# A three-block model on one core: first vectors by quarters of columns, expert weights in pieces of 16 KB, and the last scatter moved into the next stage

## The reference

```
def first_block(x, c, ctx, c_ctx, mod_w, mod_b, norm1_g, norm2_g, ...):
    for i in range(2):
        mod = silu(c) @ mod_w[i] + mod_b[i]          # 1024 -> 6 * 1024
        sh1, sc1, g1, sh2, sc2, g2 = split(mod, 6)
        mod_c = silu(c_ctx) @ mod_w[i] + mod_b[i]    # the same for the context
        h = rmsnorm(x, norm1_g[i]) * (1 + sc1) + sh1     # hc likewise
        y, yc = mixer_i(h, hc, w_qkv, w_o, ...)
        x = x + g1 * y                               # xc likewise, in layer 0
        h2 = rmsnorm(x, norm2_g[i]) * (1 + sc2) + sh2
        x = x + g2 * hier_moe(h2, ...)
    return rmsnorm(x, final_g)

def hier_moe(t, ...):     # group by argmax, 2 of the group's 8 experts by top-2
    # 32 experts, each: hidden = silu(x @ w_gate[e]) * (x @ w_up[e]); hidden @ w_down[e]
    # w_gate, w_up: 1024 x 512, w_down: 512 x 1024, each 2 MiB
```

## Time and profile before

| | us |
|---|---|
| median of 3 runs | 2894.34 (2894.28 to 2894.62) |
| profiled execution, its own time | 2893.44 |
| span of the profiled execution | 2891.6 |
| TensorE busy | 2449.8 (85%) |
| VectorE / ScalarE / GpSimd busy | 982.0 (34%) / 550.9 (19%) / 165.6 (6%) |
| DMA moved | 599.06 MB, mean 207 GB/s |

### The profile page before, as it was taken

The page is one execution under the profiler, slowest core; times in us unless marked ns, Lnnn a source line. Parts: engine busy times, 40 slices in busy tenths (PEclk is TensorE's granted clock), DMA queues, the critical chain, the costliest instruction groups (busy, mean ns, idle before and its releaser), DMA issues. The chain is left out here.

```text
span 2891.6 us, 30373 instructions
## 1 busy us (share of the span) xinstructions
PE 2449.8 (85%) x12101; PEld 1302.0 (45%) x12101; DVE 982.0 (34%) x2138; ACT 550.9 (19%) x1222; POOL 165.6 (6%) x270
## 2 busy tenths in 40 slices
PE   6999888795987777697986987777796787999999
PEld 2444356453644334344744644343343653444444
DVE  3221177654322222475734222222365342000000
ACT  3000077311100000115711100000122541000000
POOL 0000000001211111000001111111000000000000
PEclk9999999996999999898997999999898888999999
DMA  8454310507999999611057999999600123222110
GB/s 312 163 193 172 132 46 1 207 29 316 419 419 420 419 419 417 250 44 34 1 199 321 417 418 419 419 418 408 220 15 4 48 73 116 69 76 87 58 58 29
DMA packets 128449, 599.06 MB, mean 207 GB/s; under 512 B 21508, under 2 KB 23820, under 8 KB 73008
## 3 DMA queue, kind: packets, MB, share of 16 engines
q1 hardware_dynamic: 117744, 576.05, 50.3%
q0 software_dynamic: 10560, 21.01, 1.9%
HBM read 580.12 MB, written 30.51 MB: 211 GB/s over the span
## 5 line engine op out<-in xcount | busy, mean ns | idle before, releaser
L1706 PE MATMUL moe_down<-moe_wd,moe_hid_t 128*64 128x512 f32 x1024 | 238.8, 609 | 57.0 <-DMA moe_wd<-in_moe_w_down 43.9
L1661 PE MATMUL moe_gate<-moe_wg,moe_xg_t 128*64 128x256 f32 x1984 | 232.9, 388 | 55.2 <-DMA moe_wg<-in_moe_w_gate 53.7
L1661 PE MATMUL moe_up<-moe_wu,moe_xg_t 128*64 128x256 f32 x1984 | 228.9, 383 | 59.2 <-DMA moe_wu<-in_moe_w_up 59.2
L398 PE MATMUL qkv_acc<-qkv_w,a_buffer 128*128 128x512 f32 x576 | 256.2, 598 | 1.4 <-DVE a_buffer L473 1.2
L2890 PE MATMUL mlp_acc<-m_h,mlp_w 128*128 128x512 f32 x512 | 224.4, 599 | 11.4 <-DMA mlp_w<-in_w_up 9.4
L2905 PE MATMUL mlp_acc<-mlp_w,mlp_u_t 128*128 128x512 f32 x512 | 220.0, 592 | 1.4 <-DVE mlp_u_t L2925 1.4
L1661 PEld LDWEIGHTS moe_gate<-moe_wg,moe_xg_t 128*64 128x64 f32 x1984 | 148.6, 139 | 158.6 <-DMA moe_wg<-in_moe_w_gate 90.0
L1661 PEld LDWEIGHTS moe_up<-moe_wu,moe_xg_t 128*64 128x64 f32 x1984 | 147.0, 138 | 137.2 <-DMA moe_wu<-in_moe_w_up 78.3
L398 PEld LDWEIGHTS qkv_acc<-qkv_w,a_buffer 128*128 128x128 f32 x576 | 107.4, 191 | 132.7 <-issue 123.9
L2890 PEld LDWEIGHTS mlp_acc<-m_h,mlp_w 128*128 128x128 f32 x512 | 97.7, 192 | 137.7 <-issue 127.9
L1706 PEld LDWEIGHTS moe_down<-moe_wd,moe_hid_t 128*64 128x64 f32 x1024 | 73.7, 139 | 178.0 <-issue 126.1
(11 more groups left out here) (406 smaller groups left out, 2958.0 us busy)
## 6 DMA issues: line engine op xcount, KB each, us to landing
moe_wg<-in_moe_w_gate SPq DMA_DIRECT2D x64, 2048.0 KB, 34.6
moe_wu<-in_moe_w_up SPq DMA_DIRECT2D x64, 2048.0 KB, 34.5
moe_wd<-in_moe_w_down SPq DMA_DIRECT2D x64, 2048.0 KB, 34.7
qkv_mod_w<-in_mod_w SPq DMA_DIRECT2D x48, 1024.0 KB, 4.9
mlp_w<-in_w_up SPq DMA_DIRECT2D x8, 2048.0 KB, 9.1
mlp_w<-in_w_down SPq DMA_DIRECT2D x8, 2048.0 KB, 7.9
qkv_w<-in_a_w_qkv SPq DMA_DIRECT2D x12, 1024.0 KB, 9.2
moe_results<-dif_zeros SPq DMA_DIRECT2D x12, 512.0 KB, 5.2
```

What stands on the lines that cost most here:

```text
L398: mm = nc.tensor.matmul(acc[i % 4][:], h_t[:, k, t * P:(t + 1) * P], w[:, c % w_ring, k, :], start=(k == 0), stop=(k == KD - 1))
L1661: mm = nc.tensor.matmul(acc[b][halves[f], 0:HF], x_t[:, k, c, :], w[:, c, k, f * HF:(f + 1) * HF], start=(c, k) == (0, 0), stop=(c, k) == ...
L1706: mm = nc.tensor.matmul(down[b][halves[c], :], hid_t[:, k, h, :], wd[z][:, 2 * h + k, c * NCHUNK:(c + 1) * NCHUNK], start=(k, h) == (0, 0) ...
```

## The change

**A. Entry of layer 0.** Group 0's vectors are computed by quarters of 256 shift and 256 scale columns: slice z holds all 8 eighths of the contraction for 256 columns (1 MiB in 1 KB pieces), slices 0 to 5 land in the still unused buffers of q and k, and 6 and 7 in the ring. SyncE's order of loads is new; rows are loaded in pairs of tiles. The norm's sums run for tiles 0 to 3 and then 4 and 5. TensorE weaves quarters, turns of the quarters' rows, hats and the products of the first four items together. `store_rows(0)` goes. The other 40 slices are spread over items 4 to 35.

```
-    due = [later * (i + 1) // len(items) for i in range(len(items))]
+    due = [max(0, later * (i - 3) // (len(items) - 4)) for i in range(len(items))]
+    ahead = 4
+    stats = [slice(0, 4), slice(4, NT)]
...
+                if g == 0:
+                    u, side = k // 2, k % 2
+                    n0 = side * D + u * 2 * P
+                    sp.dma_start(part_slice(z), src[:, :, n0:n0 + 2 * P]).then_inc(
+                        mod_in[z % ring] if z >= 6 else early_in[z], 16)
+                    return
...
+            load_rows(0)
+            sp.dma_start(e["ident"][:], e["c_ident"]).then_inc(s["g_in"], 16)
+            load_rows(1)
...
+            load_slice(0)
+            load_slice(1)
             sp.wait_ge(s["bias_clear"], 1)
             load_bias(0)
-            load_bias(1)
-            for z in range(KD):
-                load_slice(z)
-            load_chunk(0)
+            load_half(0, 0)
+            load_slice(2)
+            load_slice(3)
+            load_rows(2)
+            load_slice(4)
+            load_slice(5)
+            load_half(0, 1)
+            load_slice(6)
+            load_slice(7)
...
+            def use_quarter(u):
+                if u >= 2:
+                    pe.wait_ge(s["mod_read"], u - 1)
+                for z in (2 * u, 2 * u + 1):
+                    pe.wait_ge(mod_in[z % ring] if z >= 6 else early_in[z], 16)
+                for k in range(KD):
+                    for j in range(4):
+                        mm = nc.tensor.matmul(mod_acc[u % 2][32 * j:32 * j + 32, 0:P], act_v[:, k, :],
+                                              part_slice(2 * u + j // 2)[:, k, quarter(j % 2)],
+                                              start=(k == 0), stop=(k == KD - 1))
...
+            def first_products(u, some):    # matmuls k = 2u, 2u+1 of the items `some`
+                for i in some:
+                    c, t = items[i]
+                    for k in (2 * u, 2 * u + 1):
...
+                        mm = nc.tensor.matmul(acc[i][:], h_t[:, k, t * P:(t + 1) * P], w[:, 0, k, :],
+                                              start=(k == 0), stop=(k == KD - 1))
...
-            for z in range(4):
-                use_slice(z)
-            for t in range(NT):
+            use_quarter(0)
+            for t in range(4):
                 turn_hat(t)
+            turn_rows(0)
+            pe.wait_ge(s["hat_read"], 8)
+            first_products(0, (0, 1))
+            use_quarter(1)
+            first_products(0, (2,))
+            turn_rows(1)
+            first_products(0, (3,))
+            first_products(1, (0, 1))
+            use_quarter(2)
...                                      # quarters 2 and 3, hats 4 and 5 likewise
+            turn_hat(5)
+            first_products(3, (0, 1, 2, 3))
```

**B. Experts' weights.** Each partition gets one piece of 16 KB from each part. So the row of a weight that meets a token column changes, and with it the order of the columns of `h` and the reads of TensorE:

```
-    rows = e["moe_w_gate"][layer].rearrange("x (c p k) n -> x p c k n", c=2, k=4)
+    rows = e["moe_w_gate"][layer].rearrange("x (p c k) n -> x p (c k n)", c=2, k=4)
...                                      # the same for up; for down:
-    rows = e["moe_w_down"][layer].rearrange("x (h p k) n -> x p h k n", h=2, k=2)
+    rows = e["moe_w_down"][layer].rearrange("x (p h k) n -> x p (h k n)", h=2, k=2)
...
-                    tr = nc.tensor.transpose(x_tp[:, k, :], xg[b][:, k:D // 2:4], e["ident"][:])
+                    tr = nc.tensor.transpose(x_tp[:, k, :], xg[b][:, k * P:(k + 1) * P], e["ident"][:])
...
-                                                  w[:, c, k, f * HF:(f + 1) * HF],
+                                                  w[:, c, k, :].rearrange(
+                                                      "p (q f j) -> p f q j", f=2, j=2)[:, f],
...
-                link(v.scalar_tensor_tensor(out, e["res"][:, t, :], n_rstd[:, one],
-                                            mul[:, side(t), :], ALU.mult, ALU.mult))
-                v.tensor_tensor(out, out, add[:, side(t), :], ALU.add).then_inc(s["h_done"], 1)
+                rows = lambda ap: ap.rearrange("p (q k) -> p q k", k=KD)
+                link(v.scalar_tensor_tensor(out.rearrange("p (k q) -> p q k", k=KD),
+                                            rows(e["res"][:, t, :]), n_rstd[:, one],
+                                            rows(mul[:, side(t), :]), ALU.mult, ALU.mult))
+                out = out.rearrange("p (k q) -> p k q", k=KD)
+                v.tensor_tensor(out, out, add[:, side(t), :].rearrange("p (q k) -> p k q", k=KD),
+                                ALU.add).then_inc(s["h_done"], 1)
```

**C. The last scatter.** It becomes the first GpSimd instruction of `enter_layer_1` and `enter_block_2`, and chunk 1 is loaded before the wait for it:

```
-            pool.wait_ge(s["idx_l_done"], 2)
-            pool.wait_ge(s["ys_in"], 16)
-            pool.wait_ge(s["y_l_done"], 1)
-            nc.gpsimd.indirect_dma_start(...).then_inc(ring["last_out"], 16)
...
+        @block.gpsimd
+        def _(pool):
+            scatter_last(nc, e, ring)
...
+            load_chunk(sp, ring, e["b_w_qkv"][0], [NCHUNK] * 3, 1)
             sp.wait_ge(ring["last_out"], 16)
-            load_chunk(sp, ring, e["b_w_qkv"][0], [NCHUNK] * 3, 1)
             sp.dma_start(ys[:], src[tiles[1]]).then_inc(s["y_in"], 16)
```

More of the change, by code:

```diff
@@ L522, in _ @@
[L522 to L524 removed]
+                modulate(k, TC + 2, s["rest_ready"])
             for j, i in enumerate(turned):
```

288 lines of the change are left out of this document (190 added, 98 removed).

## The result

The changed kernel takes 2878.53 us (median of 4 runs, 2876.04 to 2881.63) against 2894.48 before. That is 16.0 us faster; forecast were 2873 and 21. The ratio on record is 0.993, 95% interval 0.9906 to 0.9953; the two medians alone give 0.9945, inside it. A second set on another chip gave 2879.74 (2876.88 to 2884.97, 6 runs) against 2896.31, ratio 0.9935 (0.9919 to 0.9952). The profiled execution is the slowest of its four, 2881.63 us with a span of 2879.8, so its stages account for 11.8 us and not for 16. The kernel before scatters too: of its 38 runs beside the experiments, 8 took 2904.85 to 2908.09 us.

The account below looks back on a forecast made before the run. Layer 0's entry was taken as TensorE-bound from 50 us on, the experts' middle as DMA-bound, with a barrier behind each experts' stage. Terms -8 - 9 + 0.5 - 4.7 = -21.2 us gave 2873 us, range 2860 to 2888.

Parts of the forecast that it names:

- R3: Rival, entry of layer 0: the quarters' chain stalls TensorE, the new entry brings 0 to 3 us, about 2879; chance 0.13.
- R1: Rival, experts' stages: 16 KB pieces bring nothing, DMA stays at 419 GB/s, kernel at 2882 us; chance 0.15.
- Part A: Entry of layer 0: TensorE starts its QKV items sooner, four items end at 63 instead of 71.9 us; 8 us gained.
- Part B, the pieces: Experts' weight loads: 16 KB instead of 8 KB pieces lower the DMA time; 9 us gained, ends 0 and 23.
- One sign: Experts' stages: the trace was to show some 47,600 packets fewer in all.
- Part B, the moving operand: Experts' gate and up products: reading pairs of columns out of four costs zero; up to 3.6 us a block hides under DMA.
- R2: Rival, experts' stages: strided gate and up reads make TensorE the bound, kernel about 3155 to 3220 us; chance 0.12.
- Part B, the strided writes of h: Projections: two strided DVE instructions per tile delay only the last tile; +1 us, +0.5 net of shorter token turns.
- Part C: Barriers behind both experts' stages: the last scatter moved behind them saves 3.5 + 1.2 = 4.7 us, ends 0 and 6.3.
- the sentence on what is late next: Stages after the experts: rope tables may hold DVE's first head by a us; block 2's other loads stand behind the wait.

Follow-up runs that it names:

- A alone: The kernel before with only the new entry of layer 0: 2881.91 us against 2895.76 before, ratio 0.9947.
- B alone: The kernel before with only 16 KB weight pieces, permuted h and strided gate and up reads: 2887.52 us against 2896.31 before, ratio 0.9959.
- natural h: The changed kernel with h written in its natural column order and the router's weights loaded to match: 2874.55 us.
- late mul: The changed kernel with VectorE multiplying the gain into the scales after the first tile's products in both projections: 2873.62 us.
- best: The changed kernel with loads not needing the scatter ahead of its wait, later gain multiplication, and the shift vector permuted once by ScalarE: 2864.22 us.

## Why the prediction was right, and where it was not

The direction, the range and the mechanism of its two large terms were right. That the sum of 21.2 came within 5 us of 16 is partly luck: four terms were off, two gains were put too small, one gain too large and one cost too small, and they partly cancelled. The total alone would not tell the forecast from R3 (2879) or R1 (2882); the stages do.

- **Part A, taken as 8 (3 to 12): 10.6.** The start of the first item was put at 23 us and came at 25.2, the end of four items at 63 and came at 61.8. A quarter was taken as 2.4 us; the later ones take 1.96, the first took 3.64. The 2.5 us for waits and the clock weren't needed. That nothing is given back held for the stage itself and by the runs (13.9 with A alone); but part A's kernels have the small loads of layer 1 later, by 0.8 us for the rope tables and 1.1 to 2.3 us in the projection, which the prediction did not expect and no run explains.
- **Part B, the pieces, taken as 9 (0 to 23): 12.9 by the runs with pieces of 8 KB, 10.8 by their stages, 13.1 by the stages of B alone.** The line through 2 and 8 KB gave 617.9 ns, 424 GB/s; that is what was measured. The 9 was that line's 11.5, lowered for early blocks that aren't bound by DMA; the lowering was not needed. R1 is out. One sign was worked out wrongly: 47,600 pieces of 8 KB become 23,800 of 16 KB, so half as many packets go; B alone has 24,576 fewer. The Trainium skill's rule ("DMA: Bandwidth & Descriptors", "Why small descriptors are slow (HBM only)") gave an estimate of some 5 us; the runs disagree with the size.
- **Part B, the moving operand, taken as 0: 0.17 us for each of gate and up.** It hides under the DMA waits. What I had against R2, that two neighbours are read before a gap, wasn't the reason; every second column costs the same. The reason is how many of four columns are used, and with one of four R2 comes true. The Trainium skill ("SBUF — State Buffer", the note on cachelines) has full bandwidth from two hits on a line of 16 bytes and a penalty below that, for no side in particular. The runs agree with it on the moving side but for the 5%. On the weight loads they don't: there both strides cost 65 ns, and the contiguous turns of the changed kernel take 143 ns.
- **Part B, the strided writes of h, taken as +0.5 net (0 to 5): 4 by the median of natural h, and 5.6 to 9.6 longer projections by the stages, not all of it the strides'.** This is the step that failed in size. The last tiles were right in kind (+1.44 us each). Missing was the first tile of layer 1's projection: DVE's chain there starts only when the last small load lands, and no row of mine showed how little slack it had: none was waited for before, and B alone, with 1.5 us of strides and loads 0.4 later, made a wait of 0.58. I had read the waits of TensorE, and a wait that isn't there yet is in none of them.
- **Part C, taken as 4.7 (0 to 6.3): 0.** The barriers gave 4.3 and 1.6 us, close to the 4.5 and 1.8 worked out. The step that failed is the sentence on what is late next: the rope tables "may hold DVE's first head by a us", and of block 2 only that other loads stand behind the same wait. They came 2.6 and 1.8 us later, of which some 0.9 of the first are there without part C as well, at chains whose next user had 0.5 us of idle time or none, and slower products behind the waits added 1.0 and 1.6. With those loads moved the forecast term is exceeded (5.8 to 7.5).
- **R3** didn't occur: one wait of 1.07 us on the vectors' chain.

## What to carry to other kernels

Moving work behind a barrier moves whatever waits for it too: before counting the barrier's time as won, list what stands behind the moved work's semaphore on the issuing queue, and put everything that doesn't need it ahead. A longer instruction on an engine that is "34% busy" is free only where its consumer already has slack at each place; check the transposes and products that have no wait in the trace, for they can have zero slack, and here a wait of 1.8 to 2.7 us cost 3.3 to 5. And two changes that each leave a chain on time can make it late together. For a strided fp32 read of TensorE it counted here how many of four neighbours are used, and on which side the read stands.

## What the runs showed of the hardware

- Pieces of 2, 4, 8 and 16 KB ran at about 390, 410, 419 and 424 GB/s (the 4 KB from the fullest slices of short bursts): the last doubling, 8 to 16 KB, is 1.2%, in a kernel that reads 390 MB that way 12.9 us.
- A DVE instruction over 1024 fp32 columns takes 1.96 to 2.05 us with one strided operand and 1.22 to 1.29 with none, whether the strided one is the output (128 columns apart) or an input (8 apart).
- A TensorE product's moving operand costs 5% more with two of four fp32 columns used, and twice as much with one of four; a transpose's weight load of 128 columns takes 206 ns in the first case, 209 in the second and 143 contiguous (compare transposes alone: contiguous loads between products of 512 columns take 190 ns and more, as L398's 191).
- Short waits of TensorE and its clock. In layer 1's projection the 14 traces fall into three groups by the first tile's wait. Without a wait (before, late mul, best) both products behind it take 13.98 us. With 0.37 to 0.58 us (A alone, B alone, natural h) the first takes 13.98 and the second 15.68, and the profile has a stretch of it at a granted clock of 0.50, which is 1.2 GHz. With 1.8 to 2.7 us (the other eight) the first takes 15.3 to 16.9, at 0.83 for the changed kernel's 16.76, and the second 13.98. It isn't so regular elsewhere: in block 2 a wait of 1.59 us was followed by 8.75 us in the changed kernel and by 7.13, at a clock of 1.00, in late mul, and in layer 0's projection two to four of the five tiles behind the first take over 15 us behind equal waits. What decides there stays open, and so does whether this makes the changed kernel's spread of 5 to 8 us.
